# Latent attention's preparation: rotary columns as extra projected rows, one rotation of the shared key, tiled sums and factors

## The reference, cut to what matters

```python
proj = rms_norm(h, mix_norm) @ w_in
c_q, c_kv, k_rope, sb_qkv, gates = split(proj)          # 384, 256, 32, 1536, 2048 columns
q  = (rms_norm(c_q, q_latent_norm) @ w_q_up).reshape(s, 8, 96)
kv = (rms_norm(c_kv, kv_latent_norm) @ w_kv_up).reshape(s, 8, 64 + 64)
k_nope, v_mla = kv[..., :64], kv[..., 64:]
k = concatenate([k_nope, broadcast(k_rope, 8 heads)])   # one rotary part for all heads
q, k = rms_norm(q, q_head_norm), rms_norm(k, k_head_norm)   # over the 96 columns of a head
rope(x1, x2) = x1 * cos - x2 * sin, x2 * cos + x1 * sin     # on the last 32 columns of q and k
o_mla = causal_softmax_attention(q, k, v_mla)
o_sb  = stick_breaking_attention(sq, sk, sv)
merged = sigmoid(g_mla) * (o_mla @ w_branch_mla) + sigmoid(g_sb) * (o_sb @ w_branch_sb)
```

## Time and profile before

| | us |
|---|---|
| median of three runs | 1254.36 |
| the profiled execution, its time | 1254.51 |
| its span | 1252.5 |
| PE busy | 1209.8 (97%) |
| DVE busy | 879.9 (70%) |
| ACT busy | 648.2 (52%) |
| POOL busy | 231.6 (18%) |

### The profile page before, as it was taken

One profiled execution on the slowest core, in us unless ns is written; L12 is line 12 of the kernel. 1 busy time (PEld: TensorE's weight loads), 2 busy tenths in 40 slices (PEclk: granted clock), 3 DMA queues, 4 the chain that ended last, 5 costly groups with the idle time before them and its releaser, 6 DMA issues.

```text
span 1252.5 us, 19771 instructions
## 1 busy us (share of the span) xinstructions
PE 1209.8 (97%) x7890; PEld 1074.7 (86%) x7890; DVE 879.9 (70%) x1215; ACT 648.2 (52%) x858; POOL 231.6 (18%) x116
## 2 busy tenths in 40 slices
PE   5999999999999999999999999999998989999996
PEld 4888889995789988888999998888898859888885
DVE  5877766886877787766787776665578765766553
ACT  6555444560655665554643455544355764555341
POOL 1433200002000044420000015510000250445000
PEclk9999999998999999999999999999998999999998
DMA  6555555551724465555445545555576203455540
GB/s 265 205 199 184 188 189 185 196 187 49 173 106 149 160 220 187 193 202 187 175 143 201 192 176 204 178 193 201 181 257 235 102 27 108 170 202 181 189 168 34
DMA packets 31041, 217.34 MB, mean 174 GB/s; under 512 B 3408, under 2 KB 3584, under 8 KB 5488
## 3 DMA queue, kind: packets, MB, share of 16 engines
q1 hardware_dynamic: 29616, 210.66, 47.9%
q0 software_dynamic: 1344, 5.53, 1.7%
HBM read 215.10 MB, written 4.22 MB: 175 GB/s over the span
## 4 chain that ended last, share of the span: by engine, by line
PE 86%; DVE 7%; ACT 4%; issue 2%; DMA 0%; POOL 0%; DVEq 0%; SPq 0%; ACTq 0%
PE bank L1411 38%; PE bank L1412 19%; PE bank L1404 7%; PE bank L1405 7%; PE bank L1406 7%; DVE w_hl L759 2%; ACT w_hl L402 1%; PE bank L1467 1%; PE bank L1468 1%; PE bank L1469 1%; PE bank L1748 1%; PE bank L1589 1%; DVE y_f L1226 0%; PE bank L1475 0%; DVE heads L1021 0%
## 5 line engine op out<-in xcount | busy, mean ns | idle before, releaser
L759 DVE TENSOR_TENSOR w_hl<-raw,w_hl 128x2048 fp32r<-128x2048 f32 x196 | 448.7, 2291 | 113.6 <-ACT w_hl L402 112.8
L402 ACT ACTIVATE w_hl<-raw 128x2048 fp32r<-128x2048 f32 x197 | 373.7, 1901 | 121.0 <-PE bank L1406 63.1
L1411 PE MATMUL bank<-x_hl,w_hl 128*128 128x512 f32 x864 | 302.7, 396 | 12.6 <-DVE w_hl L938 12.6
L1411 PE MATMUL bank<-hidden,w_hl 128*128 128x512 f32 x864 | 299.7, 394 | 0.0
L346 POOL TENSOR_TENSOR hidden<-hid_f,hidden 128x256 fp32r<-128x256 f32 (+1 forms) x76 | 189.4, 2492 | 529.7 <-ACT hidden L489 310.7
L1412 PE MATMUL bank<-x_hl,w_hl 128*128 128x256 f32 x864 | 240.4, 278 | 0.0
L1412 PE MATMUL bank<-hidden,w_hl 128*128 128x256 f32 x864 | 239.3, 277 | 0.0
L1411 PEld LDWEIGHTS bank<-x_hl,w_hl 128*128 128x128 f32 x864 | 163.1, 189 | 50.4 <-issue 12.6
L1411 PEld LDWEIGHTS bank<-hidden,w_hl 128*128 128x128 f32 x864 | 162.0, 188 | 37.6
L1404 PE MATMUL bank<-x_hl,w_hl 128*128 128x256 f32 x576 | 166.4, 289 | 1.0 <-DVE x_hl L780 0.6
L1405 PE MATMUL bank<-x_hl,w_hl 128*128 128x256 f32 x576 | 164.3, 285 | 0.0
(11 more groups left out here) (331 smaller groups left out, 1593.1 us busy)
## 6 DMA issues: line engine op xcount, KB each, us to landing
raw<-weights SPq DMA_DIRECT2D x198, 1024.0 KB, 4.9
bias_skew<-bias_rows POOLq DMA_DIRECT2D x1, 3072.0 KB, 23.0
gate_or_bias<-bias_skew POOLq DMA_DIRECT2D x1, 2048.0 KB, 10.8
h<-x_t SPq DMA_DIRECT2D x1, 1024.0 KB, 4.9
out_t<-x_f SPq DMA_DIRECT2D x4, 256.0 KB, 2.2
con<-consts SPq DMA_DIRECT2D x1, 672.5 KB, 12.3
heads<-p_t POOLq DMA_DIRECT2D x1, 256.0 KB, 2.9
par<-small SPq DMA_DIRECT2D x1, 199.5 KB, 5.0
```

The costliest lines, as they stand in the source:

```text
L402: nc.scalar.activation(dst, src, ACT.Copy).then_inc(hi_split, 1)
L759: V.tensor_tensor(w_lo[:, s, :], raw[:, s, :], w_hi[:, s, :].bitcast(F32), ALU.subtract).then_inc(lo_split, 1)
L1411: mm(out_, w_hi[:, s, c:c + m], x, start=start, stop=False, **kw)
```

## The change

- The host packs the rotary columns of each query head a second time with their halves exchanged: a head of `q_up` has 128 output columns (64 plain, 32 rotary, 32 exchanged) instead of 96. The last latent chunk, which had 96 empty columns, holds the rotary key columns twice exchanged and twice plain.
- Cosine and sine are made in one table on 128 partitions (`angles`, `rope_tables`); sign, gain and the latent's factor are multiplied into it (`q_mult`), so that one multiplication per pair evacuates, scales and rotates the queries. Scores contract over 128 rows, cosine and sine part under each other. The shared rotary key is rotated once on DVE and copied to eight heads by ACT.
- `rotate`, POOL's cosine products and a memset of POOL are gone.
- ACT squares the projections straight from PSUM. The sums are 8 matmuls for the queries on two column tiles, 4 for the keys (two heads each) on the two others, and one for the shared rotary part. They stand before the value tokens and all gate steps.
- Key factors use two row tiles of 32 rows (partitions 64 and 96), the first two pairs before the loop, the others in its first turn.
- Gate units are cut in steps of three products: 12 and 8 steps before the loop, 16 in the first turn, 11 in each of the others, 4 behind it.
- In the head loop ACT, not DVE, copies the transposes out of PSUM. `gates_in(0)` now follows the keys; others fall in turns 0, 2, 3, 4, 6 and 7.
- POOL's bias DMAs stand right behind the first feed-forward part.

The diff, cut (a removed block of four or more lines stands as its first line and "..."; the functions are printed above). `angles` now runs one pass on 128 partitions with per-partition constants, and `rsqrt` is divided into its first line and `newton`:

```diff
-            sp.dma_start(pos_i[64:96, :], positions.partition_broadcast(32)).then_inc(pos_in, 16)
+            sp.dma_start(pos_i[:, :], positions.partition_broadcast(P)).then_inc(pos_in, 16)
...
@@ gpsimd @@
             low("ffn1")
-            for p in range(8):
...
             pool.wait_ge(bias_ready, 1)
...
@@ scalar @@
+            nc.scalar.activation(x_f[64:96, 4, :], k_rs[64:96, :], ACT.Square,
+                                 scale=float(QK) ** -0.5).then_inc(sq_ready, 1)
             for j in range(4):
                 nxt(C["sb_q"] + j)
             rsqrt("c_q")
             rsqrt("c_kv", load=False)
-            act.wait_ge(rope_ang, 2)
-            nc.scalar.activation(rope_tab[64:96, 0, :], rope_tab[64:96, 0, :], ACT.Sin).then_inc(rope_sin, 1)
-            nc.scalar.activation(rope_tab[64:96, 1, :], rope_tab[64:96, 1, :], ACT.Sin).then_inc(rope_sin, 1)
+            act.wait_ge(rope_ang, 1)
+            nc.scalar.activation(rope_keys, rope_keys, ACT.Sin).then_inc(rope_sin, 1)
             for j in range(2):
                 nxt(C["sb_v"] + j)
-            st.done(nc.scalar.activation(heads[64:96, 8:16, :],
-                                         k_rope[0:ROPE, :].rearrange("p (a b) -> p a b", a=1).to_broadcast([ROPE, 8, S]),
-                                         ACT.Copy))
+            act.wait_ge(kr_ready, 1)
+            nc.scalar.activation(heads[64:128, 8:16, :],
+                                 kr_cos.rearrange("p (a b) -> p a b", a=1).to_broadcast([64, 8, S]),
+                                 ACT.Copy).then_inc(kr_done, 1)
             for j in range(2):
+                act.wait_ge(chunk_used, C["q_up"] + j + 1)
+                for t in range(2):
+                    hd = 4 * j + 2 * t
+                    nc.scalar.activation(sq[:, hd:hd + 2, :], two(bank[:, 2 - 2 * j + t, :]),
+                                         ACT.Square).then_inc(sq_ready, 1)
                 nxt(C["q_up"] + j)
-            def head_squares(p):
...
+            act.wait_ge(k_raw, 1)
+            for t in range(2):
+                nc.scalar.activation(x_f[:, 2 * t:2 * t + 2, :], two(bank[:, 4 + t, :]), ACT.Square).then_inc(sq_ready, 1)
+            nc.scalar.preload_act_table_set("natural_log_exp_and_others")
+            rsqrt("head", load=False)
             nxt(C["kv_up"])
-            act.wait_ge(qk_raw, 10)
...
+            nxt(C["gates"])
...
@@ scalar, head loop @@
+                    act.wait_ge(m_pt, hd)
+                    if hd >= 3:
+                        act.wait_ge(m_pv, 2 * (hd - 2))
+                    nc.scalar.activation(m_t[(hd - 1) % 2], bank[:, 2, 0:384], ACT.Copy).then_inc(m_ptc, 1)
+                if hd in gate_ends:
+                    nxt(C["gates"] + gate_ends[hd])
...
@@ vector @@
+            def rope_tables():
+                dve.wait_ge(rope_sin, 1)
+                st.done(V.tensor_scalar(rope_keys, rope_keys, cst("sign", 1), None, ALU.mult))
+                dve.wait_ge(setup, 5)
+                V.tensor_copy(rope_query[64:96, :], rope_keys[64:96, :])
+                st.done(V.tensor_copy(rope_query[96:128, :], rope_keys[0:32, :]))
+                V.scalar_tensor_tensor(out=q_mult, in0=rope_query, scalar=col("q_head"), in1=r_lat[:, 0, :],
+                                       op0=ALU.mult, op1=ALU.mult)
+                for i, rows in enumerate((slice(0, 64), slice(64, 128))):
+                    V.scalar_tensor_tensor(out=lat_sq[rows, :], in0=r_lat[rows, i, :], scalar=1.0 / QK,
+                                           in1=r_lat[rows, i, :], op0=ALU.mult, op1=ALU.mult)
+                V.scalar_tensor_tensor(out=kr_cos, in0=k_rs[64:128, :], scalar=col("k_rot")[64:128],
+                                       in1=rope_keys[64:128, :], op0=ALU.mult, op1=ALU.mult)
+                st.done(V.scalar_tensor_tensor(out=kr_sin, in0=k_rs[0:64, :], scalar=col("k_rot")[0:64],
+                                               in1=rope_keys[0:64, :], op0=ALU.mult, op1=ALU.mult))
+                V.tensor_tensor(kr_cos, kr_cos, kr_sin, ALU.add).then_inc(kr_ready, 1)
...
+            rope_tables()
+            dve.wait_ge(kr_ready, 1)
             for j in range(2):
                 dve.wait_ge(chunk_used, C["q_up"] + j + 1)
                 for t in range(2):
                     hd = 4 * j + 2 * t
-                    V.tensor_tensor(heads[0:QK, hd:hd + 2, :], two(bank[0:QK, 2 - 2 * j + t, :]), lat_two[0][0:QK],
+                    dve.wait_ge(sq_ready, SQ["head"] + 2 * j + t + 2)
+                    V.tensor_tensor(heads[:, hd:hd + 2, :], two(bank[:, 2 - 2 * j + t, :]),
+                                    q_mult.rearrange("p (a b) -> p a b", a=1).to_broadcast([P, 2, S]),
                                     ALU.mult).then_inc(qk_raw, 1)
                 nxt(C["q_up"] + j)
+            dve.wait_ge(ss_ready, NO["head"] + 1)
+            st.done(V.tensor_tensor(t_a[:, :], bank[:, SUMS, 0:S], lat_sq, ALU.mult))
+            V.scalar_tensor_tensor(out=t_m[:, :], in0=t_a[:, :], scalar=EPS, in1=bank[:, SUMS, S:2 * S], op0=ALU.add,
+                                   op1=ALU.add).then_inc(ms_ready, 1)
+            def keys_in(t):
+                b = two(bank[:, 4 + t, :])
+                dve.wait_ge(sq_ready, SQ["head"] + t + 6)
+                for e in range(2):
+                    k = heads[0:NOPE, 8 + 4 * t + e:8 + 4 * t + e + 3:2, :]
+                    rows = slice(64 * e, 64 * e + 64)
+                    lat = r_lat[rows, 1:2, :].to_broadcast([64, 2, S])
+                    V.scalar_tensor_tensor(out=k, in0=b[rows], scalar=col("k_head")[rows], in1=lat, op0=ALU.mult,
+                                           op1=ALU.mult).then_inc(qk_raw, 1)
+            def normed_keys(p):
+                dve.wait_ge(bc_ready, p // 2 + 1)
+                y = heads[:, 8 + 2 * p:10 + 2 * p, :]
+                V.tensor_tensor(y, y, two(bank[:, key_bank[p], :]), ALU.mult).then_inc(normed, 1)
+            keys_in(0)
+            newton("head", t_b[:, :], r_head)
+            keys_in(1)
+            dve.wait_ge(rq_mm, 1)
+            r_q = bank[:, 0, 0:S].rearrange("p (t g i) -> p t i g", t=2, g=4)[:, :, 0:4, 0:2]
+            for dst, factor_of_q in ((q_scale, float(QK) ** -0.5), (q_minus, -float(QK) ** -0.5)):
+                V.tensor_scalar(dst.rearrange("p t (i g) -> p t i g", g=2), r_q, factor_of_q, None,
+                                ALU.mult).then_inc(rq_done, 1)
+            dve.wait_ge(kr_done, 1)
+            for p in range(2):
+                normed_keys(p)
             dve.wait_ge(chunk_used, C["kv_up"] + 1)
             for t in range(2):
                 V.tensor_scalar(mv[:, t, :], bank[:, 2 + t, :], r_tok[:, 1, t:t + 1], None, ALU.mult).then_inc(qk_raw, 1)
-            for t in range(2):
...
+            for p in range(2, 4):
+                normed_keys(p)
             def gates_in(j):
                 dve.wait_ge(chunk_used, C["gates"] + j + 1)
...
                                 ALU.mult).then_inc(drained, 1)
                 nxt(C["gates"] + j)
-            def rope(p):
...
+            nxt(C["kv_up"])
             gates_in(0)
-            for p in range(4):
...
             dve.wait_ge(rq_done, 2)
...
@@ vector, head loop @@
-                    dve.wait_ge(m_pt, hd)
...
                 if hd < HEADS:
                     dve.wait_ge(s_ln, hd + 1)
...
                     V.tensor_scalar(mp[:, 0:128], mp[:, 0:128], stat[:, 24 + o:25 + o], None, ALU.mult)
                     V.tensor_scalar(mp[:, 128:384], mp[:, 128:384], stat[:, 25 + o:26 + o], None,
                                     ALU.mult).then_inc(m_prob, 1)
-                if hd == 0:
...
+                if hd in gate_ends:
+                    gates_in(gate_ends[hd])
...
@@ tensor @@
-                    o = bank[0:QK, 2 - 2 * j + hh // 2, (hh % 2) * S:(hh % 2) * S + S]
+                    o = bank[:, 2 - 2 * j + hh // 2, (hh % 2) * S:(hh % 2) * S + S]
                     for k in range(3):
-                        last = product(o, s, k * 384 + hh * QK, QK, y_hl[:, k, :, :], k == 0, k == 2)
+                        last = product(o, s, k * 512 + hh * P, P, y_hl[:, k, :, :], k == 0, k == 2)
                 last.then_inc(chunk_used, 1)
             arrived(C["kv_up"] + 1)
             s = C["kv_up"] % RING
             for t in range(4):
                 for k in range(2):
-                    product(bank[:, 4 + t // 2, (t % 2) * S:(t % 2) * S + S], s, k * D + t * P, P, y_hl[:, 3 + k, :, :], k == 0, k == 1)
+                    last = product(bank[:, 4 + t // 2, (t % 2) * S:(t % 2) * S + S], s, k * D + t * P, P, y_hl[:, 3 + k, :, :], k == 0, k == 1)
+            last.then_inc(k_raw, 1)
+            kw = dict(skip_group_check=True)
+            for hd in range(8):
+                if hd % 2 == 0:
+                    pe.wait_ge(sq_ready, SQ["head"] + hd // 2 + 2)
+                rows = slice(32 * (hd % 2), 32 * (hd % 2) + 32)
```

(56 more changed lines are left out.)

## The result

The changed kernel takes 1244.76 us, the median of 6 runs (1244.03 to 1248.42), against 1255.71 of the kernel before in 6 runs made with them. The ratio is 0.9919, with a 95% interval from 0.9899 to 0.9938. The forecast was 1243.5, 10.9 us less than the 1254.4 shown then; these medians lie 10.95 us apart, and the two profiled executions 9.3 (1245.17 against 1254.51). In the first session of experiments the same two kernels, with four and seven runs, lie 7.6 apart (1246.93 and 1254.49). So the step is sure, and its size is known to some 2 us.

The account below looks back on a forecast made before the run. PE's program, plus the few places where it waits, was taken to set the time. Front -26.3 and loop +15.4 gave -10.9 us from 1254.4: 1243.5 us, chance 0.58, range 1238 to 1250.

Parts of the forecast that it names:

- Front: Up to the head loop's first scores: these come at 287.0 instead of 313.33, a gain of 26.3 us.
- The ACT queue: Before the sums: key copy, six squares and two splits queue behind `kr_ready`; last squares at 272.4, PE waiting from 265.2.
- The low clock: After PE's wait: last sums and half the token matmuls at half speed, 1.3 + 1.4 us more.
- the tokens: Value token matmuls behind the sums: from 275.1 to 278.6, or 2.1 us if the clock held.
- The first rival: Front and head 0: clock stays up (2.9 back), DVE reaches head 0 in time (up to 2.1); 1238.5 us, chance 0.20.
- The rule on tiling modes: PE's ten or so added mode changes: each would cost something by the rule, nearly nothing by the trace; sum left unchanged.
- Loop: Head loop with its last turn and tail: 75.3 us against 59.9 before, 15.4 more.
- Head 0: First loop turn: PE's work to 295.5, then a 2.1 us wait for DVE's first maximum at 297.6.
- Head 1: Second loop turn: 7.84 us plus a PE wait of 1.7 behind DVE's gate evacuation and split.
- The one late turn: Loop, where a gate chunk ends late (heads 4 and 7): ACT then DVE split behind it, 0.5 us of wait.
- POOL: Bias table's DMAs start near 210 and delay weight loads; taken as 0, bound 3 us.
- The third rival: Loop: weight splits become its chain, fully exposed 25 us in six iterations; slower, 1268 us, chance 0.07.

Follow-up runs that it names:

- the run with the squares first: Changed kernel with ACT's wait for the rotated key and its copy to eight heads moved behind the six squares; 1236.65 us, ratio 0.9862.
- filled wait: Changed kernel with 33 more matmuls, results overwritten, on PE while it waits for the squares; 1241.88 us, ratio 0.9903.
- the base: Changed kernel unaltered, run again beside the first experiments; 1246.93 us, ratio 0.9937.
- The run on one tile: Changed kernel with query sums, key sums and key factors each on one tile, output not the reference's; 1243.48 us, one run only.
- the run with the evacuation first: Changed kernel with DVE's next split and gate chunk 0 evacuation ahead of the last two key pairs' multiplications; 1242.51 us, ratio 0.9916.
- the run with the table late: Changed kernel with POOL issuing the bias table's DMAs only after the head loop's first maximum; 1247.19 us, ratio 0.993.
- Rotations out: Kernel before with all that only rotates left out, output not the reference's; 1242.56 us, ratio 0.9873.
- The run with both orders: Changed kernel with squares first on ACT and evacuation first on DVE together; 1234.41 us, ratio 0.9839.

## Why the prediction was right

**Front.** Forecast 26.3 us, measured 24.9. The ACT queue was worked out to the half microsecond: key copy from 263.87 (forecast 263.6), squares at 265.8, 268.7 and 271.5, last ones ready at 272.6 (272.4). That the wait is this queue, the run with the squares first shows. The low clock was sized right too: it cost 2.8 us (filled wait) for 2.7 in the sum, and 3.2 in the base, where it lasted 10.2. The term that was too small is the tokens. They ended at 279.74 for 278.6, and took 4.12 for 3.5. My sum has them at 2.1 at full clock, against the 2.75 of the row that it took them from the earlier trace rows; at full clock they took 2.86 here (filled wait). With 2.75 and the 1.4 of half speed it would have been 4.15. That slip is 0.6 of the 1.4 us by which the front was off. The rest is small: 0.2 for the squares, 0.3 for the sums behind them, and 0.3 behind the tokens. In the last two are the tiles: a pair of 32-wide matmuls takes 0.53 (1.06 for four) and not 0.44. The first rival's condition (the clock stays up) didn't come true, but where I forced it, it gave what I had priced.

**The rule on tiling modes.** I had weighed the Trainium skill, "TensorEngine Tiling (Array Packing)", section Key Properties, by which a change of tiling mode drains TensorE. The four factor matmuls, with mode changes on both sides, take 1.06 us from their first start to the next product's, 0.18 more than two paired lengths of 0.44. The run on one tile says the same: there the four, one after the other, took 1.92 to the next product's start. Four turns for two are 0.86 more, so a turn is 0.43 and 0.2 is left for both changes. By this estimate from two runs a drain, with whatever else lies there, is 0.1 us per change at most.

**Loop.** Forecast 15.4 us more, measured 14.8, and the mechanism was the forecast one. Head 0: 10.33 for 10.5. Head 1: 9.33 for 9.5. Steady turns 7.84 for 7.84. The one late turn 8.21, a wait of 0.3 for 0.5. Last turn 6.1 for 6.3. The wait of 1.7 for head 0's maximum is DVE's queue, as the run with the evacuation first shows: 2.8 us less in the loop. DVE's queue there in the changed kernel:

```profile
291.17 1.29 DVE L1021 TENSOR_TENSOR heads<-heads,bank 128x512 f32<-128x512 f32 x2 [2.95 <-PE bank L1598]
292.37 2.29 DVE L748 TENSOR_TENSOR w_hl<-raw,w_hl 128x2048 fp32r<-128x2048 f32 x1
294.57 0.68 DVE L1042 TENSOR_TENSOR gate_or_bias<-bank,r_sb 128x512 f32<-128x512 f32 x1
295.18 2.28 DVE L748 TENSOR_TENSOR w_hl<-raw,w_hl 128x2048 fp32r<-128x2048 f32 x1
```

It is idle for 2.95 us in front of the two key multiplications, with a split and an evacuation behind them that wait for nothing.

**POOL.** Forecast 0 with a bound of 3. The bias table takes 26.4 us to land now (23.0 before) and makes ACT wait 9.5 us for weights (7.0 and 2.5). In the run with the table late these two waits are gone, and PE's start of the value tokens moves by 0.1: 0.

**The third rival** (weight splits as the loop's chain) fell: DVE had room even with the copy back on it. The late turn was its only trace.

**Where the total was luck.** The front gave 1.4 us less than forecast, the loop cost 0.6 less, and behind the stage, where I had nothing, the two profiled executions differ by 1.0 the wrong way. That the medians still lie 10.95 apart for 10.9 is chance; 10.2 in the stage is what the forecast can be held to.

**What the change was worth by parts.** Rotations out: 12.6 us at the first scores. The rest of the change took 2.4 us back, 10.2 less 12.6; that is a difference of two runs, and holds if the rotations are worth the same in both kernels. It contains 8.5 us which the order of ACT's queue alone brought in (5.8 of wait and 2.8 of low clock), and 2.8 in the loop from DVE's. This was in my working as a cost; that it could be had back by moving one wait I saw only from the trace after.

## What to carry to other kernels

When a wait is put into an engine's program, list what stands behind it in that queue and who needs it: here one wait for a small copy held six squares, and with them PE, and moving it gave 8.5 us in the stage, where the whole change had given 10.2. In this kernel a low clock followed PE's waits and added a third to their price (2.8 of 8.5 us), so price a wait together with what runs behind it. Whether shorter matmuls inside a wait help must be read from the stage: in the one run with longer ones (one tile for all) the first scores came no later. The first turns of the pipelined loop were bound by what DVE's queue still held from before it (2.8 us), so put there only what the first turn needs.

## What the runs showed of the hardware

Matmuls on different tiles don't always start in program order. In the run with the squares first, all query sums (L1564) stand ahead of all key sums (L1568) in PE's program, on the other column tiles:

```profile
265.40 1.49 PE L1564 MATMUL bank<-sq,con 128*32 128x256 f32 x12
266.65 0.41 PE L1568 MATMUL bank<-x_f,con 128*32 128x256 f32 x2
266.72 0.39 PE L1564 MATMUL bank<-sq,con 128*32 128x256 f32 x2
266.89 0.39 PE L1568 MATMUL bank<-x_f,con 128*32 128x256 f32 x2
266.93 0.39 PE L1564 MATMUL bank<-sq,con 128*32 128x256 f32 x2
```

Key sums start at 266.65 and 266.89, before query sums at 266.72 and 266.93. The run with both orders shows it again (a key sum at 268.32, a query sum at 268.40). That TensorE looks ahead in this way would also explain, though it isn't shown, why the order within four matmuls made no difference to the key factors (1.06 us either way), while putting all on one tile did (1.92). How far ahead it looks wasn't tried.

The Trainium skill, "TensorE: Matmul & The Clock Gate", section Part 3: Packing small matmuls, has matmuls start and end in strict program order. For neighbours on one tile nothing here speaks against that; for different column tiles these starts do.

In the changed kernel the clock fell where PE waited, though no single wait there was longer than 2.15 us. The stretch of the sums, with the wait for squares in it, has a granted clock of 0.82, and the two behind it 0.50 and 0.67: the level of 1.2 GHz, then a mixture with 2.4. With useless products in the same wait all three were at 1.00, and so they were where the squares came first and there was no wait. A wait isn't needed, though: in the kernel before the clock was 0.62 from 290.18 on, and PE had been busy throughout the head sums and the four rotations ahead of it. How long the low clock lasts varies between executions of the same kernel: 6.8 and 10.2 us in two of the changed one, with the first scores 0.4 us apart.
